# One projection stage for the four mixer groups, operands of C and D kept in DRAM, and attention C and D each in one stage of four heads

## The reference

```
h  = rms_norm(x, norm_mix_pre)
u  = h @ w_in                                  # 1024 x 2400, cut into ua 512, ub 352, uc 768, ud 768
oa = rms_norm(gqa_axial(ua))                   # A: 4 query heads, 2 key/value heads of 64, normed, axial rotary
ob = rms_norm(mla(ub))                         # B: 192 + 128 latent columns normed, times w_uq, w_ukv; 4 heads of 96 / 64
oc = diff_attention(uc)                        # C: 4 heads, 2 maps each of 32, bias -slope*|distance|, p0 - lam*p1
od = rms_norm(neighbourhood_attention(ud))     # D: 4 heads, 8 x 16 neighbours, learned relative bias
x  = x + rms_norm(concat(oa, ob, oc, od) @ w_out)
x  = x + rms_norm(square(relu(rms_norm(x) @ w_up)) @ w_down)
```

## Time and profile before

| | us |
|---|---|
| runs | 3461.32, 3462.30, 3462.28; median 3462.28 |
| the profiled execution | 3464.52, its span 3462.8 |
| PE busy | 3078.8 (89% of the span) |
| DVE, ACT, POOL busy | 1584.9, 1271.2, 679.8 |
| DMA | 195.5 MB, mean 56 GB/s; its main queue busy 20.1% of 16 engines |
| mean granted clock of PE | 0.931 |

### The profile page before, as it was taken

How to read it: one execution, slowest core, us unless ns; L and a number is a source line. 1 busy time by engine, 2 the same in 40 slices (tenths; PEclk the granted TensorE clock), 3 DMA queues, 4 the chain that set the end, 5 groups by cost and what they waited for, 6 DMA issues and landing times. The chain is left out here.

```text
span 3462.8 us, 38563 instructions
## 1 busy us (share of the span) xinstructions
PE 3078.8 (89%) x15024; PEld 2515.7 (73%) x15024; DVE 1584.9 (46%) x2141; ACT 1271.2 (37%) x2042; POOL 679.8 (20%) x329
## 2 busy tenths in 40 slices
PE   6797788879889999999968888888889899999998
PEld 5685566768678888888757666666777788888886
DVE  4847454366642222222548366442766322222226
ACT  3556443456431111111326466333663311111114
POOL 1006340110022222222010065201100222222220
PEclk9898898889899999999979989998889999999998
DMA  6020333120231111111330312331101211111103
GB/s 158 1 70 22 90 67 67 29 64 1 73 98 48 49 49 39 47 49 49 97 68 1 91 31 59 67 67 38 56 31 62 97 49 49 43 49 49 49 25 110
DMA packets 193770, 195.54 MB, mean 56 GB/s; under 512 B 65416, under 2 KB 163720, under 8 KB 193546
## 3 DMA queue, kind: packets, MB, share of 16 engines
q1 hardware_dynamic: 193598, 193.31, 20.1%
q10 hardware_dynamic: 12, 0.02, 0.0%
HBM read 145.06 MB, written 24.89 MB: 49 GB/s over the span
## 5 line engine op out<-in xcount | busy, mean ns | idle before, releaser
L255 PE MATMUL u_ps<-h_hi,up_w_h 128*128 128x512 f32 x1024 | 408.2, 399 | 7.2 <-PEq L129 6.9
L256 PE MATMUL u_ps<-h_lo,up_w_h 128*128 128x512 f32 x1024 | 407.4, 398 | 0.0
L259 PE MATMUL u_ps<-h_hi,up_w_l 128*128 128x512 f32 x1024 | 323.8, 397 | 0.0
L2014 PE MATMUL d_ps<-wd_h,up_h 128*128 128x512 f32 x1024 | 318.4, 392 | 4.4 <-DVE m_acc L2110 2.7
L2116 DVE TENSOR_TENSOR m_square<-m_relu 128x1024 f32<-128x1024 f32 x64 | 95.2, 1487 | 492.8 <-ACT m_relu L2059 492.7
L2014 PE MATMUL d_ps<-wd_l,up_h 128*128 128x512 f32 x1024 | 315.8, 390 | 0.0
L2055 ACT ACTIVATE wd_h<-wd_raw 128x1024 fp32r<-128x1024 f32 x64 | 66.2, 1056 | 679.1 <-PE d_ps L2014 568.4
L2014 PE MATMUL d_ps<-wd_h,up_l 128*128 128x512 f32 x1024 | 315.4, 389 | 0.0
L2110 DVE TENSOR_TENSOR m_acc<-m_acc,d_ps 128x512 f32<-128x512 f32 x224 | 143.4, 683 | 370.8 <-PE d_ps L2014 364.5
L1981 POOL TENSOR_TENSOR wd_l<-wd_raw,wd_h 128x1024 fp32r<-128x1024 f32 x64 | 154.6, 2427 | 609.3 <-ACT wd_h L2055 608.8
L1975 POOL TENSOR_TENSOR up_w_l<-up_w_raw,up_w_h 128x1024 fp32r<-128x1024 f32 x62 | 172.2, 2777 | 471.6 <-ACT up_w_h L2049 471.6
(11 more groups left out here) (305 smaller groups left out, 6432.6 us busy)
## 6 DMA issues: line engine op xcount, KB each, us to landing
up_w_raw<-in_w_up SPq DMA_DIRECT2D x64, 512.0 KB, 4.3
wd_raw<-in_w_down SPq DMA_DIRECT2D x64, 512.0 KB, 3.9
wo_raw<-in_w_out SPq DMA_DIRECT2D x16, 512.0 KB, 7.2
mix<-out_x SPq DMA_DIRECT2D x16, 512.0 KB, 4.0
out_x<-mix SPq DMA_DIRECT2D x16, 512.0 KB, 4.9
mp_x<-out_x SPq DMA_DIRECT2D x16, 512.0 KB, 4.2
out_x<-mp_x SPq DMA_DIRECT2D x16, 512.0 KB, 4.9
alibi<-in_distance SPq DMA_DIRECT2D x8, 960.0 KB, 6.9
```

The source lines that it names most:

```text
L255: nc.tensor.matmul(o, w_hi, x_hi[:, tok], start=first, stop=False)
L256: nc.tensor.matmul(o, w_hi, x_lo[:, tok], start=False, stop=False)
L259: ins = nc.tensor.matmul(o, w_lo, x_hi[:, tok], start=False, stop=last)
L2014: last = nc.tensor.matmul(d_ps[:, (d0 + n) % 4, :], lhs[:, k, tok], rhs[:, k, n * HALF:(n + 1) * HALF], start=(k == 0 and rhs is d_h and l ...
```

## The change

The new code allots SBUF by hand (`Arena`) so that stages can hand operands over, and does the following in each layer:

- One `projection_stage` replaces A's, B's two and the four of C and D. Weights come in rows: 8 k-blocks of [128 x 512] for A, 8 of [128 x 352] for B, 8 of [128 x 512] for the values of C and D, through `row_raw`, a ring of two; ACT and POOL split them. PE multiplies token tile by token tile with the tokens as the stationary side, so that A and B results stand by token at once, in a ring of four PSUM banks (`row_taken`). DVE norms and rotates each tile, PE transposes it back one or two tiles later (`turn_back`), ACT and DVE split it. Values of C and D are split and sent to DRAM (`cd_v`). Then eight units of 128 columns give the queries and keys of C and D (`unit`), split and sent to DRAM (`cd_qk`). Then the heads of B as before; the first copy there waits for the spill DMAs, whose buffer it reuses.
- Attention A, then B; during B SP loads C's operands of the first two heads, stacked by the load itself. Attention C runs all four heads in one stage; SP meanwhile loads the second pair, D's bias tables and, once half of C is done, D's queries and keys. The distance table is held once; the slope enters as the scale of DVE's operation (L809 before), and C's queries carry 1/slope.
- Attention D runs all four heads; SP loads D's values and the output weights; the masking of the bias tables stands in DVE's list ahead of the maxima (`prepare`).
- `skew` of both layers is written in the first norm, behind the copy of x. Output projection and MLP have the same instructions with other SBUF addresses.

The diff, cut (most of it is moved text; helper functions of the new stage that have no part in what follows are left out):

```diff
@@ first norm, SP @@
-                    if after_loads:
-                        after_loads(sp)
+                    sp.dma_start(out, a["x"]).then_inc(x_copied, 16)
+                    for l in range(DEPTH):
+                        src = bass.AP(rel_scratch.tensor, l * REL_ROW + (REL_PAD + NA_C - GRID_W),
+                                      [[REL_C, NHEAD * REL_R], [0, GRID_W], [1, SKEW]])
+                        sp.dma_start(skew[l], src).then_inc(skew_landed, 16)
@@ projection_stage, SP @@
+                    def row(r):
+                        if r >= 2:
+                            sp.wait_ge(S["row_lo"], r - 1)
+                        for d0, c0, n in row_cols[r // KT]:
+                            sp.dma_start(row_raw[:, r % 2, d0:d0 + n], w[r % KT * P:(r % KT + 1) * P, c0:c0 + n]) \
+                                .then_inc(S[f"row_landed{r % 2}"], 16)
...
+                    for r in range(4):
+                        row(r)
+                    for dst, name in ((gc_q, "cos_a"), (gs_q, "sin_a")):
+                        sp.dma_start(dst[:, :, :], a[name].rearrange("(t p) d -> p t d", p=P)) \
+                            .then_inc(S["const_landed"], 16)
...
+                    for u in range(8):
+                        spill_unit(u)
+                        if u + 4 < 8:
+                            unit(u + 4)
+                    sp.wait_ge(S["gemm_done"], 8)
@@ projection_stage, PE @@
+                    def row_product(i, k):
+                        hi, lo = row_dst[i // NT]
+                        n = row_width[i // NT]
+                        for x, wt in ((h_hi, hi), (h_hi, lo), (h_lo, hi)):
+                            last = nc.tensor.matmul(u_ps[:, i % 4, 0:n], x[:, k, tokens(i)], wt[:, k, :],
+                                                    start=(k == 0 and x is h_hi and wt is hi),
+                                                    stop=(k == KT - 1 and x is h_lo))
...
+                    for k in range(KT):
+                        pe.wait_ge(S["row_lo"], k + 1)
+                        row_product(0, k)
+                        row_product(1, k)
+                    for i in range(2, 3 * NT):
+                        if i % NT == 0:
+                            pe.wait_ge(S["row_lo"], KT * (i // NT + 1))
+                        if i >= 4:
+                            pe.wait_ge(S["row_taken"], i - 3)
+                        for k in range(KT):
+                            row_product(i, k)
+                        if i - 2 < 2 * NT:
+                            turn_back(i - 2)
+                    for u in range(8):
+                        pe.wait_ge(S["w_lo"], u + 1)
+                        if u < 2:
+                            pe.wait_ge(S["row_taken"], 3 * NT - 2 + 2 * u)
+                        else:
+                            pe.wait_ge(S["lo_done"], u - 1)
+                        for k in range(KT):
+                            last = part_products(unit_out(u), u_h[:, u % 2, k, :], u_l[:, u % 2, k, :], h_hi[:, k, :],
+                                                 h_lo[:, k, :], k == 0, k == KT - 1)
+                        last.then_inc(S["gemm_done"], 1)
@@ projection_stage, ACT @@
+                    for r in range(KT):
+                        row_high(r)
+                    for t in range(NT):
+                        a_square(t)
+                        if t < 4:
+                            row_high(KT + 2 * t)
+                        a_root(t)
+                        if t < 4:
+                            row_high(KT + 2 * t + 1)
+                        if t >= 2:
+                            back_high(t - 2)
+                    for t in range(NT):
+                        b_square(t)
+                        if t < 4:
+                            row_high(2 * KT + 2 * t)
+                            row_high(2 * KT + 2 * t + 1)
+                        back_high(NT + t - 2)
...
+                    def query_out(e):
+                        act.wait_ge(S["q_gemm"], e + 1)
+                        if e == 0:
+                            for j in range(2):
+                                act.wait_ge(S[f"spilled{j}"], 2 * 16 * 4)
@@ attention C and D @@
-                                                       scale=1.0, scalar=MIN_START, op0=ALU.add, op1=ALU.min,
+                                                       scale=SLOPES[n // NT], scalar=MIN_START, op0=ALU.add, op1=ALU.min,
...
+            def fetch_d(sp):
+                load_c_stacks(sp, 1)
...
+                sp.wait_ge(S["scores_done"], 2 * 2 * NT)
+                sp.wait_ge(S["pv_done"], NT)
...
+                            for dst, part, is_lo in ((DQ_H, 4 + 2 * j, 0), (DQ_L, 4 + 2 * j, 1), (DK_S, 5 + 2 * j, r)):
+                                sp.dma_start(dst[d, 2 * j + h, :].bitcast(F32), cd_qk[part, is_lo, s, :].bitcast(F32)) \
+                                    .then_inc(S["copy_landed"], 16)
...
+            prepare = {0: mask_edge(0), 2: mask_inner(0)}
+            for h in range(1, NHEAD):
+                prepare[NT * h - 3] = mask_edge(h)
+                prepare[NT * h - 1] = mask_inner(h)
```

More of the change, by code:

```diff
@@ L53 @@
 SKEW = 2 * GRID_W - 1
+SLOPES = [2.0 ** (-8.0 * (h + 1) / NHEAD) for h in range(NHEAD)]
 def shape_constants():
@@ L112, in __getitem__, with __init__, take @@
         return self.by_name[name]
+class Arena:
+    def __init__(self, nc, base, *spans):
+        self.nc, self.base = nc, base
+        self.spans = [[int(lo * 1024), int(hi * 1024)] for lo, hi in spans]
+    def take(self, name, shape, dt=F32):
+        size = 4 * math.prod(shape[1:])
+        for span in self.spans:
+            if span[1] - span[0] >= size:
+                at, span[0] = span[0], span[0] + -(-size // 32) * 32
+                return self.nc.alloc_sbuf_tensor_at(name, shape, dt, offset=self.base + at)
+        raise ValueError(f"no room for {name}")
 def build(nc, a, out):
@@ L178, in build @@
         end_stage()
[L181 to L249, removed]
@@ L260, in part_products, with columns @@
             return ins
[L262 to L284, removed]
-                nc.tensor.matmul(o, hi[:, u % 2, k, :], x_hi[:, k, tok], start=(k == 0), stop=False)
-                nc.tensor.matmul(o, hi[:, u % 2, k, :], x_lo[:, k, tok], start=False, stop=False)
-                last = nc.tensor.matmul(o, lo[:, u % 2, k, :], x_hi[:, k, tok], start=False, stop=(k == KT - 1))
-            last.then_inc(S["gemm_done"], 1)
-        FULL = [(P, slice(0, KT))]
-        def full_unit(src):
-            return ([(lambda w: w, src.rearrange("(k p) n -> p k n", p=P))], FULL)
+        def columns(src):
+            return src.rearrange("(k p) n -> p k n", p=P)
         def transposes(pe, dst, src_of, n=8):
@@ L444, in attention_stage @@
+        def attention_stage(tag, mem, maps, tiles, mix_cols, mix, fetch=None, values_landed=0, prepare={}):
             n_all = len(maps) * NT
@@ L849, in difference_stage @@
             end_stage()
[L852 to L863 removed]
+        first_norm()
+        with nc.Fori(0, DEPTH) as layer:
             def vec(name, lo=None, hi=None):
@@ L1900, in build @@
+            end_stage()
             with ExitStack() as c, nc.Block() as block:
```

1996 lines of the change are left out of this document (948 added, 1048 removed).

## The result

The changed kernel takes **3242.24 us** (median, 3240.37 to 3245.49), the one before 3461.99 beside it: ratio 0.9367, 95% interval 0.9355 to 0.9378. The forecast was 3285, range 3240 to 3330: right in its direction and inside that range by 2 us, but 43 us too slow and outside the narrower range of 3265 to 3308 that its own terms gave. The profiled execution has a span of 3243.8.

What follows compares the result with a forecast made beforehand. TensorE, busy 89%, was taken as the bound, with the loss at stage ends. Per layer -99 (projection) + 8 (borders) - 11.7 (C) - 1.9 (D) = -104.6, twice -209; skew +32: -177, giving 3285 us, range 3240 to 3330.

Steps and rivals of the forecast that it cites:

- Steps 1 and 2: Projection stage, A: two tiles 24 us after first weight DMA, six more 36.9, plus 3 for clock and 3 for VectorE.
- Rival 2: Projection's row phases go at the helper engines' pace, an A tile 8.5 rather than 6.1 us: 3323 us, chance 0.14.
- Step 3: Projection stage, B's eight tiles: 33.4 us with transposes, loading of the value weights hidden.
- Step 4: Projection stage, value tiles of C and D: 45.0 us, spill DMAs hidden.
- Step 5: Projection stage, eight query and key units of C and D: 88.7 us, DMA traffic hidden.
- Steps 6 and 7: End of projection stage: 9.5 us until B's first head copy can reuse the spill buffer, then 30.9 to first score.
- Borders: Where one attention now follows another at once, three per layer: 2.7 us each, +8 per layer.
- Merging C with its border: Attention C as one stage: 11.7 us per layer saved, and 2.7 for the border avoided.
- Rival 3: Operands of C or D land late for their attentions, 20 us per layer: 3325 us, chance 0.05.
- The moved step: First norm: skew tables in SP's queue hold up layer 0's first weight rows, landing at 74 rather than 42: +32 us.
- Rival 1: The skew tables in SP's queue don't hold the weight rows up: 3253 us, chance 0.15.
- Rival 4: TensorE's clock stays at its lower level for the rest of the projection stage: 3653 us, chance 0.03.

Runs made afterwards that it cites:

- e11: e10 with A's angle tables and gains issued behind weight row 7 instead of row 3: 3230.05 us.
- e7: The changed kernel without D's bias masks, so part of the bias is not computed: 3241.65 us.
- e6: The changed kernel with C's attention as two stages of two heads instead of one: 3278.47 us.
- e4: The changed kernel with each layer's skew table written beside A's attention instead of in the first norm: 3218.80 us.
- e2: The changed kernel with pads that put h_hi, h_lo and the stages' tensors back on their old addresses: 3285.82 us.
- e3: Separate timing of dense 512-column products, other engines idle, at eight pairs of operand offsets: (0, 32) 0.2333 us, (32, 32) 0.2268 us per product.
- e8: Second table of such dense products at further offset pairs, some below 32 bytes: (16, 16) 0.2300 us, (4, 0) 0.2375 us per product.
- e10: e4 with eps_col placed ahead of ident, so that the identity too is at 160 modulo 256: 3215.68 us.

## Why the prediction was right, and where it was off

The largest term, the projection stage, was not tested by an edit of its own; it is checked below against the stretches of the new trace.

- **Steps 1 and 2** (norm to the last A tile: 73.0 forecast, 106.2 - 33.2): 70.0 in layer 1 (1649.09 to 1719.07). The start was slower than step 1: the first DMA came 7.2 us behind the norm's last matmul, not 6.0, and the two tiles were done 26.5 us behind that DMA (1656.32 to 1682.82), not 24. PE waited 4.2 us for the fifth row there. In e11, with the table DMAs behind the rows, this wait is only 1.1 us shorter (layer 0), so the term of 1 us for them was about right and most of the wait has another cause. The 6 us added in step 2 for the clock and for VectorE weren't needed: six tiles took 36.3 us, 6.12 apart, PE's own 6.14. Rival 2 is out.
- **Step 3**, B tiles: 34.2 (33.4). **Step 4**, values: 44.4 (45.0). **Step 5**, units: 86.8 to 87.0 (88.7); 384 products at 0.227 rather than 0.231. The value weights and the spills stayed hidden.
- **Steps 6 and 7**, last unit to first score: 42.6 in layer 1 and 41.3 in layer 0 (40.4). The wait for the spill was shorter than put down and the heads longer. In layer 0 the copy starts 6.8 us after the last unit:
```profile
293.47 0.39 PE L205 MATMUL u_ps_p<-b_src_h,bh_w_h 128*128 128x512 f32 x1
...
300.24 1.02 ACT L647 ACTIVATE bh_u_q<-u_ps_p 128x1024 f32<-128x1024 f32 x1 [5.54 <-DMA cd_qk<-p_l]
```
- **The stage** as a whole: 278.2 us in layer 1 against 280.5.
- **Borders**: 2.1 to 2.3 us from an attention's last matmul to the next one's first, 2.7 taken. **C** 139.7 and 139.6 (140.6). **D** 73.9 in both layers (74.6), its masks 2.7 rather than 3.5 (e7). Merging C with its border was priced at 14.4 per layer; splitting it again makes C 16.1 longer, and the time 18 per layer (e6). Rival 3 is out: no first score waits for a DMA.
- **The moved step**: the mechanism was right, the size 32 forecast, 23.4 measured (e4). The row was said to land at 74 and landed at 67.4. The order of landing is the queue's, as the sum had it: copy 33.4, tables 52.9 and 66.9, row 67.4. The mis-sized term is the tables' length: 2 x 20.5 was put down (20.5 stands in no row; the earlier trace rows have 21.8), and the first landed 19.5 us behind the copy, the second 14.0 behind the first. In e2, e6 and e7, which begin with the same DMAs, the row landed at 70.8 to 71.4, so the delay varies by some 4 us. Rival 1 (no delay) is out.
- **What was wrong** is a step that put a term at nothing: "the products themselves bring only 33.3 - 30.4 = 3 us", and the MLP, "which the change leaves alone". One pace, 0.231, was taken for old and new products. The change shifted persistent tensors, and with them the pace of all products that read h. It was in the diff (`ones` gone, `eps_col` moved) and its effect stood in the trace of before, unread: 0.234 in the up and 0.233 in the output projection against 0.227 in the down projection, at the same clock and shape. Of the 42 us of span, 23.5 are these two parts of the program and some 7, by an estimate, the projection stage's 768 long products per layer at 0.2267 rather than 0.231; 8.6 are the skew tables, the rest small terms.
- With h back in its old place (e2) the time is 3285.8 against the forecast of 3285, but that agreement is in part luck: by span it is 3280.3 against 3285.8, and 0.231 for products that with these places come 0.2333 apart made up for some of the tables' excess.
- **Rival 4**, the clock: it did not happen: the front part has 0.93 and 0.94. In the stage the clock is 1.00 from 97.0 to the last unit at 293.5 in layer 0 and from 1689 to 1885 in layer 1; it is lower at the first weight rows (0.77 and 0.76) and at B's heads (0.90 and 0.76), behind PE's idle stretches.

## What to carry to other kernels

When dense products of one shape run at two paces at the same clock, compare where their operands start; here equal places modulo 256 bytes, at multiples of 32, were the fast ones, and moving tensors by a few bytes gave 28.7 us of 3462. A diff that adds or drops one small persistent tensor moves everything allocated behind it, so put a term for that into the sum, or hold the addresses fixed while the rest is measured. A step moved to "where nobody waits for it" still stands in a queue: ask who is behind it, and look for a stage in which that queue is empty.

## What the hardware showed that was not expected

- The spacing of dense 512-column products depends on the difference of the two operands' start: 0.2267 us at 0 and 256 bytes, 0.2289 to 0.2333 at 64, 0.2322 to 0.2325 at 128, 0.2333 at 32, up to 0.2375 at 4 (e3, e8). Equal places 16 bytes behind a multiple of 32 have 0.2300. It isn't symmetric: moving 64 bytes ahead of stationary 0.2289, the other way round 0.2333. Why is left open; so is whether 128-column transposes have it (e10).
- Of two DRAM-to-DRAM writes of 1,905 KB issued one behind the other, the first took SP 1.01 us to issue and the second 29.1 (12.19 to 41.31), which also delays the end of the stage by some 3 us; the 256 KB row behind them took 16.2, where other rows take 0.33. In the kernel before, where one such write is issued behind A's short table loads, it took SP 1.08. Why the issue is held was not tried.
